# Attention by query tile with both heads of a pair together, in a streaming encoder layer

## What is computed

```python
z = einsum('bld,dc->blc', h, w_in)          # one projection: q, k, v, gates, forget logits
# 16 FoX heads (64 wide), keys of meta + prompt, causal; c = cumsum(log_sigmoid(forget))
p = softmax(where(kpos <= qpos, q @ k.T * SCALE + c_q - c_k, -1e30));  out = p @ v
# 16 sliding-window heads, 4 kv heads, relative bias, and a sink logit per head
m = max(max(s), sink);  p = exp(s - m) / (sum(exp(s - m)) + exp(sink - m));  out = p @ v
# the running stream does the same with 128 cached keys and its 64 new ones
x = LN(ALPHA * h + concat(fox * silu(gate), swa * silu(gate)) @ w_out)
```

## Time and profile before

| | |
|---|---|
| median of 3 runs | 1073.03 us (1072.53 to 1073.29) |
| the profiled execution | 1072.61 us, its span 1071.0 us |
| granted TensorE clock, mean | 0.998 |
| instructions in the trace | 20603; matmuls 7617 |

### The profile page before, as it was taken

How to read it: one execution, slowest core, us unless ns; L and a number is a source line. 1 busy time by engine, 2 the same in 40 slices (tenths; PEclk the granted TensorE clock), 3 DMA queues, 4 the chain that set the end, 5 groups by cost and what they waited for, 6 DMA issues and landing times.

```text
span 1071.0 us, 20603 instructions
## 1 busy us (share of the span) xinstructions
PE 1051.7 (98%) x7617; PEld 982.7 (92%) x7617; DVE 610.0 (57%) x1493; ACT 441.7 (41%) x1078; POOL 50.4 (5%) x99
## 2 busy tenths in 40 slices
PE   7999999999999999999999999999999999999996
PEld 6999999999999999999999999999999878888884
DVE  6655455554646455464554676554776674332486
ACT  6444444444444344444444555344554553111310
POOL 1010000000000000000000000000000000000000
PEclk9999999999999999999999999999999999999999
DMA  9142223213222212213612212122121154222413
GB/s 338 52 138 91 76 99 108 92 66 106 83 78 101 98 63 90 99 74 111 214 55 94 87 47 78 53 89 99 51 76 66 69 187 147 79 78 90 184 60 118
DMA packets 20810, 106.65 MB, mean 100 GB/s; under 512 B 3216, under 2 KB 3632, under 8 KB 11488
## 3 DMA queue, kind: packets, MB, share of 16 engines
q1 hardware_dynamic: 14960, 83.13, 21.9%
q0 software_dynamic: 5808, 22.95, 6.4%
HBM read 95.18 MB, written 14.17 MB: 102 GB/s over the span
## 4 chain that ended last, share of the span: by engine, by line
PE 91%; DVE 4%; issue 2%; ACT 0%; DMA 0%; SPq 0%; DVEq 0%; ACTq 0%
PE ps L1145 59%; PE ps L1294 19%; PE ps L1264 5%; PE ps L1242 4%; PE ps L1226 2%; PE ps L1225 2%; DVE small L889 1%; DVE tb L875 1%; PE ps L1175 1%; PE ps L1278 1%; DMA x_raw<-in_xT 0%; DVE small L902 0%; DVE small L900 0%; DVE tb L906 0%; SPq L476 0%
## 5 line engine op out<-in xcount | busy, mean ns | idle before, releaser
L1145 PE MATMUL ps<-xh,wh 128*128 128x288 f32 (+1 forms) x1664 | 506.5, 304 | 0.5 <-DVE wl L948 0.5
L1145 PE MATMUL ps<-xl,wh 128*128 128x288 f32 (+1 forms) x1664 | 493.5, 297 | 0.0
L1145 PE MATMUL ps<-xh,wl 128*128 128x288 f32 (+1 forms) x1664 | 493.1, 296 | 0.0
L1145 PEld LDWEIGHTS ps<-xh,wh 128*128 128x128 f32 x1664 | 313.6, 188 | 9.6 <-issue 7.2
L1145 PEld LDWEIGHTS ps<-xl,wh 128*128 128x128 f32 x1664 | 313.9, 189 | 0.0
L1145 PEld LDWEIGHTS ps<-xh,wl 128*128 128x128 f32 x1664 | 313.5, 188 | 0.0
L798 DVE TENSOR_TENSOR wl<-w_raw,wh 128x1024 fp32r<-128x1024 f32 x132 | 160.2, 1221 | 80.8 <-ACT wh L619 79.8
L1294 PE MATMUL ps<-wh,mix_parts 128*128 128x512 f32 x576 | 185.4, 391 | 0.0
L619 ACT ACTIVATE wh<-w_raw 128x1024 fp32r<-128x1024 f32 x132 | 138.0, 1054 | 77.4 <-PE ps L1294 70.3
L667 ACT ACTIVATE tb<-tb,small 128x256 f32<-128x256 f32 (+5 forms) x160 | 82.6, 516 | 206.5 <-DVE small L885 130.7
L1294 PEld LDWEIGHTS ps<-wh,mix_parts 128*128 128x128 f32 x576 | 108.2, 188 | 22.5 <-DVE mix_parts L1013 0.3
(11 more groups left out here) (112 smaller groups left out, 844.8 us busy)
## 6 DMA issues: line engine op xcount, KB each, us to landing
w_raw<-in_w_all SPq DMA_DIRECT2D x66, 1024.0 KB, 4.8
cbc<-c_rows POOLq DMA_DIRECT2D x16, 360.0 KB, 4.1
x_raw<-in_xT SPq DMA_DIRECT2D x7, 592.0 KB, 10.0
rows<-in_x_p POOLq DMA_DIRECT2D x4, 1024.0 KB, 5.1
out_y_p<-rows SPq DMA_DIRECT2D x16, 256.0 KB, 2.5
rel_copies<-rel_rows POOLq DMA_DIRECT2D x1, 3072.0 KB, 13.0
out_fvT<-vT POOLq DMA_DIRECT2D x8, 296.0 KB, 2.4
out_fkT<-kT POOLq DMA_DIRECT2D x8, 296.0 KB, 2.5
```

The costliest lines, as they stand in the source:

```text
L1145: ins = nc.tensor.matmul(ps[:, st.bank(k, h), 0:width], a[k % 2][:, w], b[:, ko, first:first + width], start=(ko == 0 and i == 0), stop=(k ...
```

## The change

The unit of work is now a query tile `i` (0 to 4) with both heads. Scores of the two heads are made in one step, into two banks side by side (four for the two pieces of FoX tile 3; in the final stretch the two halves of one bank). For Swa the bias is added for both heads in one instruction, for FoX the decay still per head; the mask, the maxima, the minimum with the sink, the sum with it and the reciprocal are one instruction each for both. `exp` and the scaling stay one per head. All turned blocks of both heads are copied by one instruction. The meta keys come first in every tile: those of both heads (2 x 16 columns) are written side by side in `tb_meta`, turned by one transpose and copied once, and multiplied with a `v_nat` block whose rows hold the meta values of head 0 (rows 0 to 15) and head 1 (16 to 31), the other head's part being zero. For that ACT writes the meta columns of v twice (`v_twice`), and DVE multiplies the turned block by a mask (`own_meta`, made by POOL at the start). `tb` holds two tiles of two heads (four rows as before), `pt` two tiles. A stretch's steps are now: long, score at 3i+2; short and final, score at 2i+1; turn 4 steps after the score everywhere; values 3 steps after the turn, but 1 step after it in the final stretch.

The core of the diff (the lines taken away are printed above):

```diff
-        if final:
-            score, turn, value = [[u + c for u in range(10)] for c in (1, 4, 5)]
-        elif self.steps >= 32:
-            score = [min(2 * u + 2, u + 9) for u in range(10)]
-            turn, value = [[x + c for x in score] for c in (4, 7)]
+
+
+        if self.steps >= 32:
+            score = [3 * i + 2 for i in range(5)]
         else:
-            score = [u + 1 for u in range(10)]
-            turn, value = [[min(u + c, self.steps - 1) for u in range(10)] for c in (4, 7)]
+            score = [2 * i + 1 for i in range(5)]
+        turn = [x + 4 for x in score]
+        value = [x + 5 if final else min(x + 7, self.steps - 1) for x in score]
...
+            def probabilities(st, i):
+
+                tile, n = QTILE[i], 5 * st.g + i + 1
...
+                for head in range(2):
+                    t, nm = tb[:, i % SLOTS, head, 0:st.kind.keys(tile)], neg_max[:, i % 3, head:head + 1]
+                    nc.scalar.activation(t, t, ACT.Exp, bias=nm, accum_out=total[:, i % 3, head:head + 1]
+                                         ).then_inc(exp_done, 1)
+                    if st.kind is Swa:
+                        nc.scalar.activation(sink_exp[:, i % 3, head:head + 1], sink_pair[:, head:head + 1], ACT.Exp,
+                                             bias=nm).then_inc(sink_done, 1)
+
+            def keep_turned(st, i):
+
+                tile, n = QTILE[i], len(st.kind.turned_blocks(QTILE[i]))
+                if i >= 2:
+                    act.wait_ge(valued, 5 * st.g + i - 1)
+                act.wait_ge(turned, 5 * st.g + i + 1)
+                ins = nc.scalar.activation(pts[i % 2][:, :, 0:n, :], st.turned_of_both(ps, n), ACT.Copy)
+                if st.kind.meta(tile):
+                    ins = nc.scalar.activation(pt_meta[0:2 * N_META, i % 2, :], st.turn_meta_out(ps, n), ACT.Copy)
+                ins.then_inc(turned_read, 1)
...
+                    for i in st.at(st.score_at, s - 1):
+                        probabilities(st, i)
+                    for i in st.at(st.turn_at, s - 1):
+                        keep_turned(st, i)
...
+            def scores(st, i):
+
+                tile, n = QTILE[i], 5 * st.g + i + 1
...
+                        for head in range(2):
+                            ins = nc.vector.scalar_tensor_tensor(
+                                out=rows_[:, head, a:b], in0=st.score_out(ps, head, piece, b - a),
+                                scalar=cqp[:, i, head:head + 1], in1=cbc[:, head, c0:c0 + b - a], op0=ALU.add,
+                                op1=ALU.subtract)
...
+                            ins = nc.vector.tensor_tensor(rows_[:, :, to:to + n_keys],
+                                                          st.scores_of_both(ps, to, to + n_keys),
+                                                          bias[:, :, c0:c0 + n_keys], ALU.add)
...
+                nm = neg_max[:, i % 3, :]
...
+                    nc.vector.tensor_reduce(nm, rows_[:, :, 0:keys], AX, ALU.max, negate=True).then_inc(max_ready, 1)
...
+                    nc.vector.tensor_reduce(nm, rows_[:, :, 0:keys], AX, ALU.max, negate=True).then_inc(max_raw, 1)
+                    dve.wait_ge(max_raw, n - 5 * FOX_PAIRS)
+                    nc.vector.tensor_tensor(nm, nm, neg_sink, ALU.min).then_inc(max_ready, 1)
+
+            def reciprocals(st, i):
+
+                n = 5 * st.g + i + 1
+                t, rc = total[:, i % 3, :], recip[:, i % 3, :]
+                dve.wait_ge(exp_done, 2 * n)
...
                 nc.vector.reciprocal(rc, t).then_inc(recip_done, 1)
-
-                row = tb[:, u % SLOTS, 0:st.kind.keys(QTILE[UNITS[u][0]])]
                 dve.wait_ge(recip_done, n)
-                nc.vector.tensor_scalar(row, row, rc, None, ALU.mult).then_inc(scaled, 1)
+                first = 0
+                if st.kind.meta(QTILE[i]):
+                    first = N_META
+                    nc.vector.tensor_tensor(tb_meta[:, i % SLOTS, :].rearrange("p (h n) -> p h n", h=2),
+                                            tb[:, i % SLOTS, :, 0:N_META],
+                                            rc.rearrange("p (h o) -> p h o", o=1).broadcast_to([P, 2, N_META]), ALU.mult)
+                for head in range(2):
+                    row = tb[:, i % SLOTS, head, first:st.kind.keys(QTILE[i])]
+                    nc.vector.tensor_scalar(row, row, rc[:, head:head + 1], None, ALU.mult).then_inc(scaled, 1)
...
+            def score(st, i):
+
+                tile = QTILE[i]
...
+                for piece, (a, b) in enumerate(pieces):
+                    p = st.kind.first(i) + piece
+                    if piece:
+                        pe.wait_ge(v_ready, 4 * st.kvs)
+                    elif p:
+                        pe.wait_ge(score_read, st.kind.base(st.g) + p)
+                    for head in range(2):
+                        if i == 0 and piece == 0:
+                            pe.wait_ge(k_doubled, 4 * st.kvs - 1 + head)
+                            pe.wait_ge(k_split, 4 * st.kvs - 1 + head)
+                        queries = q2[:, head * NQ + P * tile:head * NQ + P * (tile + 1)]
+                        out = st.score_out(ps, head, piece, b - a)
+                        nc.tensor.matmul(out, queries, k2[:, head, a:b], start=True, stop=False)
+                        ins = nc.tensor.matmul(out, queries, k_low[:, head, a:b], start=False, stop=True)
+                    ins.then_inc(scored, 1)
+
+            def turn(st, i):
+
+                tile, n = QTILE[i], 5 * st.g + i
...
+                else:
+                    pe.wait_ge(turned_read, n)
+                for head in range(2):
+                    pe.wait_ge(scaled, 2 * n + head + 1)
+                    for j, (first, _) in enumerate(blocks):
+                        ins = nc.tensor.transpose(st.turn_out(ps, head, j), tb[:, i % SLOTS, head, first:first + P],
+                                                  ident[:])
+                if st.kind.meta(tile):
+                    ins = nc.tensor.transpose(st.turn_meta_out(ps, len(blocks)), tb_meta[:, i % SLOTS, :], ident[:])
+                ins.then_inc(turned, 1)
...
+            def values(st, i):
+
+                tile = QTILE[i]
+                blocks = [(pts[i % 2][:, :, j, :], v) for j, (_, v) in enumerate(st.kind.turned_blocks(tile))]
+                if st.kind.meta(tile):
+                    both = pt_meta[:, i % 2, :].rearrange("p (o q) -> p o q", o=1).broadcast_to([P, 2, P])
+                    blocks.append((both, Values.META))
...
+                pe.wait_ge(turned_read, 5 * st.g + i + 1)
```

More of the change, by code:

```diff
@@ L72 @@
 TILE_STEPS = OUT_STEPS // 4
-UNITS = [(index, head) for index in range(5) for head in range(2)]
 QTILE = [3, 2, 1, 0, 4]
@@ L99, in bias_runs, with blocks, copies, first @@
     return [(a, b, buckets[a]) for a, b in zip(cuts, cuts[1:])]
-class Fox:
-    PIECES = 12
+class Values:
+    META, NEW_KEYS, CACHED = 0, 5, 6
+    @staticmethod
+    def blocks():
+        return ([(0, N_META)] + [(N_META + P * j, P) for j in range(3)], [(N_META + 3 * P, P), (NEW, DEC_SEQ)])
+    @staticmethod
+    def copies():
+        return (P, 1, 3, 0, 1), (P, 4, 1, 1, 0), (DEC_SEQ, V_NEW, 1, 1, 1)
+class Fox(Values):
+    PIECES = 6
     @staticmethod
     def base(g):
-        return 12 * g
+        return 6 * g
     @staticmethod
-    def first(u):
-        return 2 * u if u < 2 else u + 2
+    def first(i):
+        return i + 1 if i else 0
     @staticmethod
@@ L122, in blocks, with turned_blocks, meta, first @@
     @staticmethod
[L123 removed]
+    def turned_blocks(tile):
         if tile == 4:
[L129 to L132 removed]
+            return [(0, V_NEW), (DEC_SEQ, V_CACHE)]
+        return [(N_META + P * j, j + 1) for j in range(tile + 1)]
     @staticmethod
[L135 to L147 removed]
+    def meta(tile):
+        return tile < 4
+class Swa(Values):
+    PIECES = 5
     @staticmethod
     def base(g):
[L151 removed]
+        return 5 * g + FOX_PAIRS
     @staticmethod
[L154 to L155 removed]
+    def first(i):
+        return i
     @staticmethod
@@ L643, in evacuate @@
                         act.wait_ge(lf_stored, 16)
+                    if tile == "v" and h == 0:
+                        meta = ps[:, st.bank(k, h), 0:N_META].rearrange("p (o n) -> p o n", o=1)
+                        nc.scalar.activation(v_twice[:].rearrange("p (o n) -> p o n", o=2),
+                                             meta.broadcast_to([P, 2, N_META]), ACT.Copy)
                     nc.scalar.activation(dst[:, first:first + width], src, ACT.Copy).then_inc(evacuated[h], 1)
@@ L916, in keep_values @@
             def keep_values(st):
-                for rows_, b0, n, bank, j in st.own.value_copies():
+                dve.wait_ge(v_turned, 2 * st.kv + 1)
+                mask = own_meta[0:2 * N_META, :].rearrange("p (h o) -> p h o", o=1).broadcast_to([2 * N_META, 2, HD])
+                nc.vector.tensor_tensor(v_nat[0:2 * N_META, Values.META, :].rearrange("p (h c) -> p h c", h=2),
```

(20 more changed lines are left out.)

243 lines of the change are left out of this document (90 added, 153 removed).

## The result

The changed kernel takes 1077.16 us in the median of 6 runs (1077.0 to 1077.61), the one before 1072.67 beside it (6 runs, 1072.4 to 1073.29): a ratio of 1.0041, 95% interval 1.0028 to 1.0054. It is 4.5 us slower; forecast was 3.2 us slower than the 1073.03 shown, 1076.2.

What follows compares the result with a forecast made beforehand. PE, busy in 98% of the span, was taken as the bound. Terms -4.4 - 0.4 + 4.0 + 2.2 + 1.75 = +3.15 us on 1072.6 give 1075.8; with the median 0.4 higher, 1076.2 us, range 1068.5 to 1080.

Steps and rivals of the forecast that it cites:

- Transposes, -4.4: On PE, 40 fewer transposes of meta keys at 0.11 us each save 4.4 us.
- The 2.2 us estimated from the Trainium skill: Alternative saving for the 40 transposes on PE, from the skill's matmul pace of 56 ns for 128 columns.
- Grouping, -0.4: PE's start-up is 0.05 us cheaper where values and a turn share a step; 9 x 4 against 7 x 4 meetings.
- The short stretch, +1.25 each: PE waits 1.25 us at the second turn for ACT's copy; four ordinary stretches, less old waits, +4.0 us.
- Keys, 0.7 in each of two stretches: In short stretches after new keys, PE waits 0.7 us for the second head's keys at the first scores.
- The final stretch, 1.0, 0.45 and 0.95 of waits: PE's waits in us before the first, second and third values, for ACT's copy of the turn; sum 2.4.
- The term +1.75: Net cost of the final stretch in us: new waits of 2.4 less the old 0.66.
- Long stretches, no waits: PE does not wait in long stretches; both heads of FoX tile 3 are scaled in time, 0.6 us to spare.
- The thinnest cover, at tile 3: In long stretches, FoX tile 3's scaling finishes 0.6 us before PE needs the second head; repeats nine times.
- DVE's lag, 0.5 us from gates and weights: In short stretches DVE starts the second tile's scores late, at 623.3, where PE had them ready at 622.7.
- the half-wait rival: New waits come at half size, ordinary ones 0.75 us without DVE's lag: 1071.9 us, no change; chance 0.27.
- The merged instructions end the waits: Rival: ACT's copy is done before PE's second turn, likewise at the final values, so no new waits: 1064.8 us; chance 0.13.

Runs made afterwards that it cites:

- meta_twice: The changed kernel with each transpose of the meta block issued twice, 416 transposes in all: 1082.07 us.
- copy_first_meet: copy_first with the values of a tile in short and final stretches moved to the step of the next tile's turn: 1063.67 us.
- copy_first: The changed kernel with ACT's copy of a turned tile called ahead of the two heads' exps in a step that has both: 1065.78 us.
- gates_late: The changed kernel with the gates of the earlier pair multiplied on DVE at step 4 of short stretches: 1076.51 us.
- gates_early: The changed kernel with the gates of the earlier pair multiplied on DVE at step 0 of short stretches: 1077.8 us.
- copy_first_last_pair: copy_first with the fourth tile's values in short stretches moved to step 15, directly ahead of the fifth's: 1063.36 us.

## Why the prediction came out as it did

**Transposes, -4.4: right.** 40 fewer, 0.11 us each by meta_twice, for full and narrow blocks alike. The 2.2 us estimated from the Trainium skill (VectorE: DVE Perf Modes, the section on the TRN2 errata) is half of it; page and measurement differ, and the measurement decides.

**Grouping, -0.4: right in price, by counting.** The 0.05 us per meeting was confirmed by copy_first_meet, and long stretches took back 0.61 us where four transposes and four meetings make 0.64. What I did not see is the larger neighbour of this term: a lone group of values costs some 0.35 us more than one joined to another. It did not enter this change, which leaves their number alone. POOL got four instructions more, not five (103 against 99), and no wait for them shows. The extra work at the v tiles, costed at nothing, was not priced by a run of its own; by these prices 0.03 us in a long stretch are all that is left for it.

**The short stretch, +1.25 each: right in mechanism, 0.14 too low.** The adds of the first three tiles on DVE, and the second tile's exp on ACT:

```profile
615.05 0.69 DVE L901 TENSOR_TENSOR tb<-ps,bias 128x512 f32<-128x512 f32 x1 [0.53 <-PE ps L1265]
...
619.43 0.69 DVE L901 TENSOR_TENSOR tb<-ps,bias 128x512 f32<-128x512 f32 x1
...
623.49 0.68 DVE L901 TENSOR_TENSOR tb<-ps,bias 128x512 f32<-128x512 f32 x1
```

```profile
621.07 0.51 ACT L701 ACTIVATE tb<-tb,small 128x256 f32<-128x256 f32 x1 [0.35 <-DVE small L918]
```

Counted from the first tile's add at 615.05 the chain ran so: second scores at 4.38 us (forecast 4.37), second exp 6.02 (6.0), third scores 8.44 (8.4), third exp 10.08 (10.0), copy done 12.02 (12.0), PE ready 10.76 (10.8). Every step was within 0.11 us. The missing 0.13 is the time from the copy's end at 627.07 to the transpose at 627.20, which I left out here (in the last short stretch this step takes only 0.05, yet the wait is 1.41 there too). Six waits of 1.40 instead of four of 1.25 and two of 1.3 are 0.8 us of the 1.3 us by which the forecast fell short of the measured slowdown (4.5 against 3.2).

Two small things in these stretches had no term and nearly cancel. The pauses of 0.05 us that copy_first took away add 0.1 to nearly each. And without any wait an ordinary stretch takes 33.74 us in copy_first against 34.09 before, 0.35 less, where the old wait that is gone (0.30), the transpose (0.11) and the lost meetings (0.20) make 0.21: a saving of 0.14 whose source no run isolates. The third turn was forecast to find its copy 0.2 us earlier than the second; on the stretch shown the copy ends at 631.99 and the turn starts at 632.12, as close as behind a wait. It did not wait, but it had nothing to spare.

**Keys, 0.7 in each of two stretches: too high.** The second head's scores waited 0.55 us, on top of the 0.24 that the first head's waited before as well (timeline of PE after):

```profile
578.62 0.28 PE L1265 MATMUL ps<-k_low,q 128*128 128x256 f32 x1
579.28 0.36 PE L1264 MATMUL ps<-k,q 128*128 128x256 f32 x1 [0.39 <-DVE k_low L855]
```

From 578.62 to 579.28 are 0.66 where 0.12 is normal. This took 0.3 us off the sum in the two stretches.

**The final stretch, 1.0, 0.45 and 0.95 of waits: 1.29, 0.58 and 0.95.** At the first, from the last score product at 864.53 on, DVE's part took 2.03 us where I had 1.94, the exps 1.49 (1.40), the copy 0.60 (0.58) and the handover 0.14 (0.05): small amounts of one sign in a series make 0.3. At the second and third the handover took the 0.05 that I had. The third came out as worked out. The term +1.75 was mis-sized; it measured 2.82 - 0.66 = 2.16. So the waits in the short stretches (+0.8), the keys (-0.3) and this term (+0.4) make 0.9 of the 1.0 us by which PE's path, 4.1 us longer, missed the sum of 3.15; the medians of the runs differ by 0.4 more than the path does.

**Long stretches, no waits: right.** All eight FoX stretches shrank alike, by 0.59 to 0.61. The thinnest cover, at tile 3, was a little thicker than the forecast's 0.6 us: in the third long stretch both heads are scaled by 208.09 and PE comes to the second head at 208.99, so 0.9 us are left.

**DVE's lag, 0.5 us from gates and weights:** gates_late found 0.31 of it due to the gates, but taking it away brought the turn forward by 0.1 only. As a term it is therefore not additive: the half-wait rival (waits of 0.75 without the lag) had the same fault, since another step of the chain is next.

**The merged instructions end the waits (1064.8):** this did not happen by itself, but one exchange of two calls on ACT made it happen, and gave 1065.8. The condition that the rival named, the copy done before PE comes to the second turn, was the right one.

## What to carry to other kernels

When units of work are merged, look at what each in-order engine has queued ahead of the piece that the critical engine waits for. Here the merged exps had taken the place of one, the maximum that they waited for came later, and a copy whose input was long ready stood behind them; calling the ready work first cost nothing and gave back 11.4 us. A busy share says nothing on this: ACT was idle for over 1 us right ahead of the blocking exp.

On a bound TensorE, count how often its stream of long products is broken, not only what breaks it. Each lone group of small matmuls cost some 0.35 us more than a joined one, with no wait in any list; the time from start to start shows it, the idle time does not.

## What the runs showed of the hardware

- A transpose of float32 costs 0.11 us of PE whether it has 16 columns (before), 32 (meta_twice) or 128 (both), at a granted clock of 0.996 to 0.998.
- One DVE instruction over two PSUM banks (512 elements) takes 0.69 us, where two over 256 took 0.42 each.
- From the end of ACT's copy to the start of the matmul that waited for it pass 0.13 us in five of the six short stretches and 0.14 at the first values of the final one, but 0.05 in the last short stretch and at the second and third values; gates_early and gates_late show the same. What makes the two sizes is not shown.
- Around a lone group of values PE loses 0.1 us ahead of it and 0.1 on the first product behind it (copy_first). Transposes directly behind it give back 0.05 to 0.06 in short stretches (copy_first_meet); joining two groups gave back 0.33 to 0.39 (copy_first_last_pair).
